# One scheduler for the order of all stages of the attention and retention phase, in place of an interleave per step

## The reference, cut to what matters

```python
qa, ka, va, qr, kr, vr, g_ret, gate_a, gate_r = mix_inputs(xp, w_in[l], g_mix_norm[l], g_q_norm[l], g_k_norm[l], pos_p)
o_a = diff_out(diff_attn_prompt(qa, ka, va, lam), g_sub_norm[l], lam_init)
o_r, s_fin = retention_prompt(qr, kr, vr)
o_r = ret_out(o_r, g_ret, g_ret_norm[l])
...
# merge_and_tail
mix = jax.nn.sigmoid(gate_a) * o_a + jax.nn.sigmoid(gate_r) * o_r
x = x + mix @ w_o
h = rmsnorm(x, g_ffn)
x = x + (jax.nn.silu(h @ w_ff_gate) * (h @ w_ff_up)) @ w_ff_down
```

## Time and profile before

| | |
|---|---|
| runs, us | 4071.26, 3913.57 |
| the profiled execution, us | 3907.75 |
| its span on the core shown, us | 3906.2 |
| spans of the 8 cores, us | 3888.1 to 3906.2 |
| mean granted TensorE clock | 0.822 to 0.827 |
| PE busy in phase B (198 to 3075 us) | 2104.3 of 2877 us |
| ACT busy in phase B | 1479.7 |
| DVE busy in phase B | 1202.4 |
| POOL busy in phase B | 884.3 |

### The profile page before, as it was taken

The page is one execution under the profiler, slowest core; times in us unless marked ns, Lnnn a source line. Parts: engine busy times, 40 slices in busy tenths (PEclk is TensorE's granted clock), DMA queues, the critical chain, the costliest instruction groups (busy, mean ns, idle before and its releaser), DMA issues.

```text
span 3906.2 us, 76412 instructions; the slowest of 8 cores (3888.1 to 3906.2 us)
## 1 busy us (share of the span) xinstructions
PE 2811.9 (72%) x18314; PEld 1615.7 (41%) x18314; DVE 1535.7 (39%) x5097; ACT 1720.6 (44%) x5876; POOL 1016.5 (26%) x2668
## 2 busy tenths in 40 slices
PE   1167766776677677767867776777678579975997
PEld 1134443454345334434543453445345334432443
DVE  3244334444434444444444443443444233332343
ACT  4245544563455356445634553564456221132103
POOL 1132233233323322332332232222323110111111
PEclk9977887797778778877877886788778789987998
DMA  5631163135114411531351154115112654516551
GB/s 169 162 80 48 46 84 71 49 56 86 57 40 73 79 48 46 85 70 48 57 88 56 43 73 75 48 46 76 49 47 51 96 100 66 71 42 131 76 79 46
DMA packets 338116, 274.93 MB, mean 70 GB/s; under 512 B 165072, under 2 KB 264528, under 8 KB 337552
## 3 DMA queue, kind: packets, MB, share of 16 engines
q0 software_dynamic: 222640, 103.63, 21.4%
q1 hardware_dynamic: 115040, 166.41, 14.1%
HBM read 328.23 MB, written 36.70 MB: 93 GB/s over the span
## 4 chain that ended last, share of the span: by engine, by line
PE 60%; ACT 14%; issue 10%; DVE 10%; DMA 3%; POOL 2%; SPq 1%; DVEq 1%; ACTq 0%; POOLq 0%
PE psum L673 12%; PE psum L1031 8%; PE psum L846 7%; PE psum L614 5%; PE psum L1208 4%; PE psum L1212 4%; PE psum L825 4%; PE psum L1223 4%; ACT PT L854 3%; PE psum L685 2%; DMA Kc<-ck 2%; PE psum L930 2%; PE psum L1238 2%; DVE trT L616 1%; PE psum L1179 1%
## 5 line engine op out<-in xcount | busy, mean ns | idle before, releaser
L846 PE MATMUL psum<-QTz,KT 128*128 128x256 bf16 x2176 | 518.8, 304 | 244.2 <-ACT PT L854 202.4
L673 PE MATMUL psum<-WA,hTA 128*128 128x448 bf16 x2112 | 658.8, 393 | 41.2 <-DMA hTA<-hT_scr 41.2
L854 ACT ACTIVATE PT<-psum 128x512 bf16<-128x512 f32 x960 | 569.5, 599 | 39.7 <-PE psum L825 20.2
L825 PE MATMUL psum<-V,PT 128*128 128x129 bf16 x4096 | 478.2, 238 | 30.4 <-ACT PT L857 14.9
L1033 ACT ACTIVATE cm_E<-psum 128x384 f32<-128x384 f32 x136 | 66.8, 491 | 958.3 <-PE psum L1031 951.8
L825 PEld LDWEIGHTS psum<-V,PT 128*128 128x128 bf16 x4096 | 332.7, 106 | 106.9 <-issue 40.1
L846 PEld LDWEIGHTS psum<-QTz,KT 128*128 128x128 bf16 x2176 | 195.7, 105 | 381.7 <-issue 332.7
L1031 PE MATMUL psum<-WC,hTC 128*128 128x384 bf16 x1088 | 341.7, 488 | 0.0
L994 POOL CAST Sbf<-S 64x128 bf16<-64x128 f32 x128 | 37.2, 291 | 1068.4 <-DVE cm_rl L1037 732.8
L673 PEld LDWEIGHTS psum<-WA,hTA 128*128 128x128 bf16 x2112 | 212.1, 106 | 176.4 <-issue 84.5
L970 DVE TENSOR_TENSOR AT<-psum,DT 128x128 bf16<-128x128 f32 x128 | 37.3, 291 | 585.3 <-PE psum L967 536.7
(11 more groups left out here) (163 smaller groups left out, 5367.2 us busy)
## 6 DMA issues: line engine op xcount, KB each, us to landing
hTA<-hT_scr SPq DMA_DIRECT2D x264, 256.0 KB, 3.4
hTC<-hT_scr SPq DMA_DIRECT2D x136, 256.0 KB, 3.4
Kc<-ck POOLq DMA_DIRECT2D x32, 512.0 KB, 10.1
Vc<-cv POOLq DMA_DIRECT2D x32, 512.0 KB, 11.8
Wg<-w_g POOLq DMA_DIRECT2D x20, 512.0 KB, 5.7
Wu<-w_u POOLq DMA_DIRECT2D x20, 512.0 KB, 8.2
xt<-x_own SPq DMA_DIRECT2D x17, 512.0 KB, 4.5
k_own<-knf SPq DMA_DIRECT2D x136, 64.0 KB, 1.6
```

What stands on the lines that cost most here:

```text
L673: P.op("pe", lambda e, kt=kt: e.matmul(pA, lhsT=hTt[:, kt, :], rhs=wa[:, kt, :], start=(kt == 0), stop=(kt == 7)), [hTtb, wab], [pAb])
L825: P.op("pe", lambda e, kbi=kbi, lb=lb, m=m, stt=stt, fin=fin: e.matmul(pOa[:, m * 129:(m + 1) * 129], lhsT=PT_ap_fn(kbi, m), rhs=V_t[:, lb ...
L846: P.op("pe", lambda e, kbi=kbi, lb=lb: e.matmul(pS[set_][:, kbi * 256:(kbi + 1) * 256], lhsT=KT_t[:, lb * 128:(lb + 1) * 128], rhs=QT2, st ...
L854: P.op("act", lambda e: e.activation(out=PT[:, 0:n * 256], in_=pS[set_][:, 0:n * 256], func=AF.Exp, scale=0.125), [B("pS", set_)], [PTb])
```

## The change

The stages themselves are unchanged, and so is every operation in them. All stages of all 136 pairs are recorded first. Then one loop orders them. A stage becomes active when the stages that its `gates` name are finished (all of their operations issued), and the loop takes one operation at a time from the active stages by the old cost with one more term, 1500 for each pair by which a stage is younger than the oldest active one. C of pair t becomes active when B and B2 of pair t are done, where before it stood in the loop step behind; A of pair t may start when B and B2 of pair t - 2 are done, even if A2 of pair t - 1 is still open.

```diff
--- before.py
+++ after.py
@@ -1071,27 +1071,69 @@
     fetch_hTA(*seq[0])
     states = [dict() for _ in seq]
     n = len(seq)
+    ent = {}
+
+    def cap(kind, t, fn, *args):
+        P.begin()
+        fn(*args)
+        ent[(kind, t)] = dict(ops=P.end(), pos=0)
+
     for step in range(n + 2):
-        lists = []
         if step < n:
-            P.begin()
-            stA(seq[step][0], seq[step][1], states[step], seq[step + 1] if step + 1 < n else None)
-            lists.append(P.end())
-            P.begin()
-            stA2(seq[step][0], seq[step][1], states[step])
-            lists.append(P.end())
+            cap("A", step, stA, seq[step][0], seq[step][1], states[step], seq[step + 1] if step + 1 < n else None)
+            cap("A2", step, stA2, seq[step][0], seq[step][1], states[step])
         if 1 <= step <= n:
-            P.begin()
-            stB(seq[step - 1][0], seq[step - 1][1], states[step - 1])
-            lists.append(P.end())
-            P.begin()
-            stB2(seq[step - 1][0], seq[step - 1][1], states[step - 1])
-            lists.append(P.end())
+            t = step - 1
+            cap("B", t, stB, seq[t][0], seq[t][1], states[t])
+            cap("B2", t, stB2, seq[t][0], seq[t][1], states[t])
         if step >= 2:
-            P.begin()
-            stC(seq[step - 2][0], seq[step - 2][1], states[step - 2])
-            lists.append(P.end())
-        P.interleave(lists)
+            t = step - 2
+            cap("C", t, stC, seq[t][0], seq[t][1], states[t])
+
+    def gates(kind, t):
+        if kind == "A":
+            return [("A", t - 1), ("B", t - 2), ("B2", t - 2)]
+        if kind == "A2":
+            return [("A2", t - 1), ("A", t - 1), ("B", t - 2), ("B2", t - 2)]
+        if kind == "B":
+            return [("A", t), ("A2", t), ("B", t - 1), ("C", t - 2)]
+        if kind == "B2":
+            return [("A", t), ("A2", t), ("B2", t - 1), ("C", t - 2)]
+        return [("B", t), ("B2", t), ("C", t - 1)]
+
+    def finished(key):
+        e = ent.get(key)
+        return e is None or e["pos"] >= len(e["ops"])
+
+    pending = sorted(ent.keys(), key=lambda k: (k[1], k[0]))
+    active = []
+    while pending or active:
+        still = []
+        for k in pending:
+            if all(finished(g) for g in gates(*k)):
+                if ent[k]["ops"]:
+                    active.append(k)
+            else:
+                still.append(k)
+        pending = still
+        if not active:
+            assert not pending, "scheduler gate deadlock"
+            break
+        ratios = {k: ent[k]["pos"] / len(ent[k]["ops"]) for k in active}
+        rmin = min(ratios.values())
+        est = {k: P._peek(ent[k]["ops"][ent[k]["pos"]][0]) for k in active}
+        tmin = min(est.values())
+        age = min(k[1] for k in active)
+        bk = min(active, key=lambda k: (est[k] - tmin) + 4000.0 * (ratios[k] - rmin) + 1500.0 * (k[1] - age))
+        e = ent[bk]
+        for (kind_, args, kw) in e["ops"][e["pos"]]:
+            if kind_ == "op":
+                P.op(*args, **kw)
+            else:
+                P.dma(*args, **kw)
+        e["pos"] += 1
+        if e["pos"] >= len(e["ops"]):
+            active.remove(bk)
     dbg("mixT", mixT[:, :, :], [128, NH, NOWN * 128], BF16, [B("mixT", lb) for lb in range(NOWN)])
```

## The result

The changed kernel takes **4451.56 us** (median of 11 runs; its fastest 4446.53), the kernel before 3903 to 3914 in the undisturbed ones of its runs (3908 is used below): ratio **1.142, 95% interval 1.135 to 1.148**, so some 540 us slower. Slower was forecast with 0.85; 4145 us was forecast, with a range up to 4260, and the loss is more than double the forecast one. The profiled execution has a span of 4444.5 us, its granted clock is 0.813.

A forecast was written before the change was run, and what follows sets the result against it. No engine is full; ACT idles 121.4 us a head until stage C's matmuls L1031 are done. Order terms of 15.5 and a clock term of 14.3 give 29.8 a head, 238 over 3907.75: 4145 us, range 3985 to 4260.

The forecast's parts named there:

- The loop: In every pair the next attention's scores wait for all of stage C; a step takes 15.6 + 0.6 i us.
- Lead: From stage C's eight matmuls L1031 to the transpose of `mixb`: 7.9 us, of which TensorE waits 6.42; can't be shorter.
- `mixb` to the first score: From the transpose of `mixb` through those of `qnb` and `rbf` to the first score: 3.7 us a step.
- The sample pair: Last pair of a head: 46.1 us against 41.4, +4.7, with the 2.3 us wait for keys gone.
- The weights': Five weight DMAs hold POOL ahead of casts into `rbf`: 2.5 us in seven heads of eight, +2.2 a head.
- first score to the next C8: Attention up to stage C's next matmuls L1031: 0.6 us per exponential, 2.4 for A2's ACT part, 1.6 rest.
- The clock: Attention begins at 1.2 GHz for 4.5 us: 1.1 us in 13 steps, 14.3 us a head.
- Rival 1: The scores wait for stage C in every step, but the clock holds: 4032 us; chance 0.27.
- Rival 2: Faster: `mixb` transpose ready 4.4 us after stage C's L1031 start, steps 3.5 shorter, 3584 us; turns at 6.9; chance 0.05.
- Rival 3: No change: A2's part hides in TensorE's waits, 1 us less in 13 steps a head, 3928 us; chance 0.10.
- Rival 4: Worse: casts, copies and exponentials in order block each other, another 1 us a step, 4249 us; chance 0.08.

The follow-up runs named there:

- fillers_throughout: Changed kernel plus 16 unread matmuls ahead of each `mixb` transpose and two behind each of five lone transposes, pairs' fillers not in sample pairs; 4396.72 us, ratio 1.125.
- loop_open_mid: Changed kernel with one gate added: stage C of pair t starts only when A and A2 of t+1 are through; 4101.03 us, ratio 1.049.
- short_c_changed: Changed kernel with stage C shortened: T1 to T4 left out, `mixb` is An + Rn, not the reference's result; 4121.98 us, ratio 1.051.
- fillers_in_wait: Changed kernel plus 16 unread matmuls of 384 columns per pair, except sample pairs, on TensorE just ahead of the `mixb` transpose; 4452.59 us, ratio 1.139.

## Why the prediction was wrong in size

**The loop** was read rightly from the order, and its two first links held. Lead (C8 to `mixb`): 7.9 forecast, 7.8 at the median of the steps with C8 at 2.4 GHz and 9.1 where C8 itself runs at 1.2, as at 1687.50; 131.2 us a head for 126.4. `mixb` to the first score: 3.7 forecast, 3.84 at i = 9; 68.4 for 65.2. The waits stand where they were named: 3.60 us before `mixb` (3.5 to 4 forecast), 2.3 before L1033 (2), the clock at 0.50 at the first scores. C8 was to take 1.5 us throughout; it often doesn't (2.73 at i = 3 and i = 9). The intervals between C8 came out longer than named: 21.97 us at i = 3 and 26.63 at i = 14, where 17 and 24 to 25 were named, growing by 0.5 a block and not by 0.6 or more.

**The sample pair** came to 46.6 us for 46.1, and the wait of 2.3 for keys is gone there, as forecast. **The weights'** 2.2 us a head don't show: behind their DMAs the wait of the first transpose of `rbf` is 0.93 (at 1114.70), and 0.90 in a step without them (at 1698.65). The eight L673 that the forecast itself put behind `mixb` in this step, at 1.2 GHz, last as long as the DMAs (to 1113.7) and cover them.

**The step that failed is "first score to the next C8"**, 4.0 + 0.6 i with the clock's 1.1 on top. Measured is 7.6 + 0.51 i (a line through i = 3 to 14, mean of all cores): 9.0 for 6.9 at i = 3, 11.9 for 10.5 at i = 9. 30.5 us a head are missing, and the runs divide them so:
- The clock was sized nearly right: 18.8 us a head for 14.3, so 4.5 of the 30.5.
- **A2 on TensorE** had no term. The prediction priced A2 by its 2.4 us on ACT and never counted its eight L673 and eight L685 between the groups: 8 x 448 + 8 x 192 = 5120 columns, 2.1 us at 2.4 GHz, twice that at 1.2. Three fifths of these columns, taken out with the clock held, were worth 160.6 - 145.7 = 14.9 us a head.
- 11.1 remain (145.7 for 134.6 without the clock term), and their cause stays open. ACT's two last waits in the step shown, 0.16 and 0.61, would make 10.8 over 14 steps; that is one step's reading, not a test. The two fifths of A2's columns that stayed in would, at the same price, be worth 9.9 (an estimate, 14.9 x 2 / 3); no run takes them out.

Why the old order had not paid for them I read from the earlier trace rows and its counterpart: before, ACT waited 4.8 us a head for scores. It had stage C's part of 3.1 us and A's besides, with which to fill the gaps while TensorE did L673. The change took stage C out of the attention, and I credited all of it as a shorter queue on ACT. No run was made for this, but two traces bear it out in part. Taken from the first score to the last value matmul of each block, in us per head as in the table, fillers_throughout needs 152.7, with ACT busy for 109.5 and idle for 43.2. loop_open_mid, whose clock in the first 4.5 us is nearly as high (0.89 for 0.94), has the same instructions of ACT in this stretch and stage C's besides: it needs 175.4, with ACT busy for 149.7 and idle for 25.6. So of 40.2 us of stage C 17.6 fall into waits of ACT and cost nothing; only 22.7 lengthen the stretch. The two orders differ in more than that, so this is a comparison and not a test, and it looks at the same missing 26 us from ACT's side. The prediction took over "ACT sets the pace" from a stretch in which ACT had a third kind of work, and did not ask whether it still would.

**The rivals.** Rival 1 (the clock holds, 4032) names a real term, but with the clock held (0.913) the time is 4397. Rival 2 (faster, turning at a lead of 6.9 us) got little weight rightly, but its turning point is wrong: short_c_changed has a lead of 7.0 (112.5 / 16) and is still 5% slower than before, where the rival's own sum has next to no change at that lead. Rival 3 had A2's part hide in TensorE's waits; the contrary happened. Rival 4 (engines block each other in order, 13 us a head more than the forecast) came nearest to the mechanism, without naming A2's matmuls, and was priced at a third of the missing 36.7 and given 0.08.

In the Trainium skill (Perfetto Trace Analysis, Matmul Optimizations) it is important that matmuls execute back-to-back in batches, because power follows use. The trace agrees with the mechanism: filled waits lift the clock from 0.813 to 0.865 and 0.913. The time hardly follows (0 and 50 us): the first doesn't lift it at the scores, and the second wins 18.8 us a head there and loses 13.0 elsewhere.

## What to carry over

When work is moved out of a stretch, ask of both sides of each handshake what that work had covered: the engine that paces a stretch may do so only because it never runs out. In a loop through an engine that works in program order, first move what doesn't need the awaited result ahead of the wait (here 310 us for two transposes a step), and only then shorten the waited chain. A weight that orders "older work first" puts the longest chain in front of the next independent work: try it at several values, since here 0 to 200 gave 6 to 7% less than before and 1500 gave 14% more.

## What the runs showed of the hardware

Filler matmuls can take the low level away from where it costs little and leave it where it costs. In the changed kernel at i = 9 it lasts from 1697.2 to 1704.1, over the lone transposes and the first scores. With the wait filled (fillers_in_wait) it lasts from 1707.0 to 1710.5: it was still 1.00 through the lone transposes, which have little use for it, and fell with the first scores, which need it. A chain of small transposes costs 0.68 us a piece at the upper level (fillers_in_wait, from 1705.12 to 1705.80) and 0.75 at the lower (the rows of `rbf` above): most of it is TensorE's wait of 0.47 for the copy.
